# All expert slots gathered ahead of the first expert of a two-block network in fp32 on one NeuronCore

## The reference, cut to what matters

```python
probs = jax.nn.softmax(h @ router_w, axis=-1)            # 16 experts in 4 groups
best_group = jnp.argmax(group_score, axis=-1)            # one group for each token
# two experts of that group, with weights that sum to one -> combine
for e in range(N_EXPERTS):
    he = (jax.nn.silu(h @ w_gate[e]) * (h @ w_up[e])) @ w_down[e]
    out = out + combine[:, e:e + 1] * he
```

## Time and profile before

| | |
|---|---|
| median of 3 runs | 1371.65 us (1367.9 to 1377.59) |
| the profiled execution's own time | 1371.72 us |
| its span | 1370.4 us |
| the small gather | 975.57 to 981.43 us |
| gate sums, slot weights and up sums of the first expert | 981.43 to 1006.57 us |
| the large gather | 1006.57 to 1013.65 us |

### The profile page before, as it was taken

One profiled execution on the slowest core, in us unless ns is written; L12 is line 12 of the kernel. 1 busy time (PEld: TensorE's weight loads), 2 busy tenths in 40 slices (PEclk: granted clock), 3 DMA queues, 4 the chain that ended last, 5 costly groups with the idle time before them and its releaser, 6 DMA issues.

```text
span 1370.4 us, 20186 instructions
## 1 busy us (share of the span) xinstructions
PE 1296.8 (95%) x7932; PEld 1162.0 (85%) x7932; DVE 1021.1 (75%) x1456; ACT 707.8 (52%) x977; POOL 0.4 (0%) x5
## 2 busy tenths in 40 slices
PE   6988999999999999999999899999899999999996
PEld 6877899999888888999998688988788878878775
DVE  5667777777677897878887858775758679688695
ACT  3433444554358873554454544332557567566564
POOL 0000000000000000000000000000000000000000
PEclk9978999999999999999999999999899999999998
DMA  8628788686376766767771732220458869788781
GB/s 339 261 64 325 268 324 304 241 310 238 130 297 256 256 236 253 263 229 255 268 249 52 248 106 77 93 74 1 175 170 314 303 231 341 253 291 298 232 302 67
DMA packets 82688, 308.20 MB, mean 225 GB/s; under 512 B 9313, under 2 KB 9569, under 8 KB 81825
## 3 DMA queue, kind: packets, MB, share of 16 engines
q1 hardware_dynamic: 80352, 292.59, 59.4%
q10 hardware_dynamic: 2240, 14.31, 2.7%
HBM read 305.82 MB, written 1.05 MB: 224 GB/s over the span
## 4 chain that ended last, share of the span: by engine, by line
PE 69%; DVE 18%; DMA 7%; ACT 4%; issue 2%; ACTq 0%; SPq 0%; DVEq 0%
PE ps L468 68%; DMA ring<-stream 5%; DVE w_low L427 4%; DVE junk L427 3%; ACT w_high L427 1%; DMA ring<-moe 1%; DVE ti L427 1%; DVE rs L427 1%; DVE x L427 1%; DVE hsc L427 1%; DVE t_two L427 1%; PE ps L1138 1%; DVE x_low L427 1%; DVE y_experts L427 1%; ACT t_two L427 1%
## 5 line engine op out<-in xcount | busy, mean ns | idle before, releaser
L427 DVE TENSOR_TENSOR w_low<-ring,w_high 128x1024 fp32r<-128x1024 f32 x368 | 442.2, 1222 | 140.1 <-ACT w_high L427 138.3
L427 ACT ACTIVATE w_high<-ring 128x1024 fp32r<-128x1024 f32 x368 | 386.1, 1058 | 300.4 <-PE ps L468 173.9
L468 PE MATMUL ps<-x_high,w_high 128*128 128x256 f32 (+1 forms) x816 | 239.1, 293 | 18.6 <-DVE x_low L427 12.0
L468 PE MATMUL ps<-x_high,w_low 128*128 128x256 f32 (+1 forms) x816 | 235.9, 289 | 0.0
L468 PE MATMUL ps<-x_low,w_high 128*128 128x256 f32 (+1 forms) x816 | 235.5, 289 | 0.0
L427 DVE CUSTOM_DVE_ANT_0 junk<-ring,cond 128x1024 f32<-128x1024 f32 x137 | 167.1, 1223 | 39.6 <-DMA ring<-stream 30.9
L468 PEld LDWEIGHTS ps<-x_high,w_high 128*128 128x128 f32 x816 | 155.8, 191 | 25.9 <-issue 12.0
L468 PEld LDWEIGHTS ps<-x_low,w_high 128*128 128x128 f32 x816 | 155.8, 191 | 1.6
L468 PEld LDWEIGHTS ps<-x_high,w_low 128*128 128x128 f32 x816 | 155.2, 190 | 1.7
L468 PE MATMUL ps<-h_high,w_high 128*128 128x256 f32 x512 | 144.7, 283 | 7.1 <-DVE h_low L427 4.8
L468 PE MATMUL ps<-h_high,w_low 128*128 128x256 f32 x512 | 144.7, 283 | 0.0
(11 more groups left out here) (324 smaller groups left out, 1962.1 us busy)
## 6 DMA issues: line engine op xcount, KB each, us to landing
ring<-stream SPq DMA_DIRECT2D x364, 512.0 KB, 5.3
ring<-moe SPq DMA_DIRECT2D x192, 512.0 KB, 4.8
gw<-gw ACTq DMA_DIRECT2D x1, 3840.0 KB, 16.0
tab_two<-tab ACTq DMA_DIRECT2D x1, 2824.0 KB, 15.4
cond<-cvec ACTq DMA_DIRECT2D x2, 512.0 KB, 5.4
x<-xT ACTq DMA_DIRECT2D x1, 1024.0 KB, 11.7
ctx_first<-ctxT ACTq DMA_DIRECT2D x1, 1024.0 KB, 4.9
ctx<-ctxT ACTq DMA_DIRECT2D x1, 1024.0 KB, 4.9
```

The source lines that it names most:

```text
L427: return op(*a, **k).then_inc(self.sem, by)
L468: return pe.matmul(out, stationary, moving, start=start, stop=stop, skip_group_check=True)
```

## The change

PE does the large gather directly after the small one, and only then the first gate sums, which now wait for all 12 copies of either kind. ScalarE and VectorE take the eight copies of the large gather directly behind the four of the small one, and split the first four weight pieces in between, one after every second copy of the large gather, where before they split one after each copy of the small one. `rows_of_slots` stands behind the second gate piece of the first expert instead of the first. The waits for `scat` and `cw` that stood ahead of the large gather are gone; `products` waits for `cw` in its place. Numbers of instructions are as before on each engine.

```diff
@@ -1073,13 +1073,14 @@
     def rows_of_slots():
 
         pe.wait_ge(s.diag, 2)
-        pe.wait_ge(s.xg_high, 2)
+        pe.wait_ge(s.xg_high, 12)
         for b in range(2):
             ins = mm(PS[:, 5, b * P:(b + 1) * P], m.ONES, m.DIAG[:, b, :], True, True)
         ins.then_inc(s.db_mm, 1)
 
     def weights_of_slots():
         pe.wait_ge(s.comb_w, 1)
+        pe.wait_ge(s.xg_low, 12)
         for i in range(5):
             for b in range(2):
                 ins = mm(PS[:, 7, 4 * i:4 * i + 4], m.ONEHOT[:, b, i * P:(i + 1) * P].bitcast(F32), m.ROUT[:, 848 + 4 * b:852 + 4 * b], b == 0, b == 1)
@@ -1087,8 +1088,6 @@
 
     def other_tokens():
 
-        pe.wait_ge(s.scat, 5)
-        pe.wait_ge(s.cw, 1)
         for k in range(KT):
             pe.wait_ge(s.xg_high, 4 + max(k - 1, 0))
             tokens(PS[:, 4 + k % 2, 0:CAP - 256], 0, k, slice(256, CAP)).then_inc(s.xg_mm, 1)
@@ -1102,12 +1101,9 @@
         pe.wait_ge(s.w_low, split_upto(w + 1))
         for a, tile in enumerate(tiles_of(p)):
             for k in (2 * n, 2 * n + 1):
-                if p == 0 and kind == "g" and a == 0 and k % 2 == 0:
-                    pe.wait_ge(s.xg_high, n + 1)
-                    pe.wait_ge(s.xg_low, n + 1)
-                if p == 1 and kind == "g":
-                    pe.wait_ge(s.xg_high, 4 + k + 1)
-                    pe.wait_ge(s.xg_low, 4 + k + 1)
+                if p == 0 and kind == "g" and (n, a) == (0, 0):
+                    pe.wait_ge(s.xg_high, 12)
+                    pe.wait_ge(s.xg_low, 12)
                 slots = slice(tile * P, (tile + 1) * P)
                 ins = mm3(PS[:, (0 if kind == "g" else 2) + a, :], (m.XGH[:, k, slots], m.XGL[:, k, slots]), weight(w, (k % 2) * 512, 512), k == 0, k == KT - 1)
         ins.then_inc(s.used, 1)
@@ -1122,7 +1118,7 @@
                     pe.wait_ge(s.y_add, Y_SUMS[p - 4])
         for n in range(first, last):
             hidden(p, "g", n)
-            if p == 0 and n == 0:
+            if p == 0 and n == 1:
                 rows_of_slots()
             if p in SCATTERS:
                 scatter(SCATTERS[p], n)
@@ -1173,10 +1169,10 @@
                     ins = mm(out, m.YS[n][:, blk], m.SCAT[:, i + 1, :], n == 0, n == 1)
         ins.then_inc(s.sc_mm, 1)
 
+    other_tokens()
     gate(0, 0, 4)
     weights_of_slots()
     up(0)
-    other_tokens()
     for p in range(NE):
         if p < NE - 1:
             head = 1 if EXPERTS[p + 1][0] == 0 else 2
@@ -1613,7 +1609,11 @@
     for r in range(4):
         act.wait_ge(s.xg_mm, 2 * r + 1)
         A(m.XGH[:, 2 * r:2 * r + 2, 0:256], PS[:, XG_BANKS[r][0], :].rearrange("p (k s) -> p k s", k=2), ACT.Copy, s.xg_high, apart=True)
-        high_upto(W_MOE + r + 1)
+    for k in range(KT):
+        act.wait_ge(s.xg_mm, 8 + 2 * k + 1)
+        A(m.XGH[:, k, 256:CAP], PS[:, 4 + k % 2, 0:CAP - 256], ACT.Copy, s.xg_high, apart=True)
+        if k % 2:
+            high_upto(W_MOE + k // 2 + 1)
 
     def signs(p):
         for a in range(len(tiles_of(p))):
@@ -1652,9 +1652,6 @@
     high_upto(W_MOE + 8)
     signs(0)
     high_upto(W_MOE + 12)
-    for k in range(KT):
-        act.wait_ge(s.xg_mm, 8 + 2 * k + 1)
-        A(m.XGH[:, k, 256:CAP], PS[:, 4 + k % 2, 0:CAP - 256], ACT.Copy, s.xg_high, apart=True)
     for p in range(NE):
         w = MOE_AT[p, "d", 0] - 4
         high_upto(w + 5)
@@ -2362,12 +2359,16 @@
     def first_low(r):
         vv.wait_ge(s.xg_mm, 2 * r + 2)
         op(vv.tensor_copy, m.XGL[:, 2 * r:2 * r + 2, 0:256], PS[:, XG_BANKS[r][1], :].rearrange("p (k s) -> p k s", k=2), inc=s.xg_low, apart=True)
-        low_upto(W_MOE + r + 1)
 
     first_max(ML, NE, EX, st[:, 34:36], TM)
     op(vv.scalar_tensor_tensor, ML, EX, -3e30, ML, ALU.mult, ALU.add)
     for r in range(4):
         first_low(r)
+    for k in range(KT):
+        vv.wait_ge(s.xg_mm, 8 + 2 * k + 2)
+        op(vv.tensor_copy, m.XGL[:, k, 256:CAP], PS[:, 6 + k % 2, 0:CAP - 256], inc=s.xg_low, apart=True)
+        if k % 2:
+            low_upto(W_MOE + k // 2 + 1)
     first_max(ML, NE, E2, st[:, 36:38], TM)
     op(vv.tensor_tensor, EX, EX, E2, ALU.add)
     op(vv.tensor_tensor, EX, EX, PR, ALU.mult)
@@ -2387,6 +2388,8 @@
 
     def products(p):
         vv.wait_ge(s.used, MOE_AT[p, "u", 3] + 1)
+        if p == 0:
+            vv.wait_ge(s.cw, 1)
         for a, tile in enumerate(tiles_of(p)):
             vv.wait_ge(s.silu, tiles_upto(p - 1) + a + 1)
             if p > 0:
@@ -2428,9 +2431,6 @@
             add_branch(d, PS[:, LAST_BANKS[r] if i == 3 else 6 + r % 2, (d % 2) * 256:(d % 2 + 1) * 256], m.MOD[:, 136 + d:137 + d])
 
     low_upto(W_MOE + 12)
-    for k in range(KT):
-        vv.wait_ge(s.xg_mm, 8 + 2 * k + 2)
-        op(vv.tensor_copy, m.XGL[:, k, 256:CAP], PS[:, 6 + k % 2, 0:CAP - 256], inc=s.xg_low, apart=True)
     products(0)
     for p in range(NE):
         w = MOE_AT[p, "d", 0] - 4

```

## The result

The changed kernel takes 1375.66 us (median of 20 runs, 1371.91 to 1381.27), the one before 1370.74 us (20 runs, 1367.5 to 1377.59). The ratio is 1.0036, 95% interval 1.0026 to 1.0046, which is 3.6 to 6.3 us more: a small loss, but clear of the noise. The profiled execution took 1376.15 us, its span is 1374.9 us.

What follows compares the result with a forecast made beforehand. PE was taken to bound the kernel (busy 95% of the span, 69% of the chain that ended last). The terms -7.08 + 10.1 + 0.7 = +3.7 us gave 1375.4 us from 1371.72, with a range of 1370.5 to 1380.5.

Steps and rivals of the forecast that it cites:

- Part A: Large gather leaves its old place between first up sums and second gate, wholly on PE's path: -7.08 us.
- Part B: Large gather ahead of the first gate, which waits until VectorE finishes eight copies and three splits: +10.1 us.
- Part C: Hand-over from first to second expert: without the gather's cover, PE waits for products before the transposes: +0.7 us.
- Parts at nothing: Later `scat` operations, router's small operations, `rows_of_slots`, the `cw` wait and later first four splits: no cost.
- Rival 1: Clock falls in the new gather's pauses and stays low past the gate's start: 1377 to 1379 us; chance 0.27.
- The rule of the Trainium skill: Cycling through PSUM banks with small pauses between matmul groups can swing the clock; first gate sums would start slow.
- Rival 2: VectorE's splits and copies hide under PE, so the large gather runs at PE's pace: 1371.2 to 1371.8; chance 0.09.
- Rival 3: Expert weight stream falls behind in one-tile experts, PE waits a few times: +4 to +6, 1380 us; chance 0.07.
- signs of being wrong: Gate before 989 or after 994, PEclk under 1.00 after 991, or ScalarE's one-tile `ring<-moe` wait much over 1 us.

Runs made afterwards that it cites:

- e6: Kernel before, large gather in its old place, ScalarE and VectorE making the split of the second gate's last piece behind the eight copies; ratio 1.0000.
- e4: Changed kernel, with VectorE doing each of the three low splits between the large gather's copies an extra time into spare memory; ratio 1.0078.
- e2: Changed kernel, with VectorE making all eight copies of the large gather first and the four low splits behind them; ratio 1.0024.
- e3: Changed kernel, with VectorE making the first expert's products ahead of the low split of the second gate's last piece; ratio 1.0032.
- e1: Changed kernel, with the first gate sums waiting for 4 copies of either kind instead of 12; ratio 1.0020.
- e5: Changed kernel with the edits of e1 and e3 together; ratio 1.0029.
- e10: e1 profiled once more, unchanged, to see whether its low clock comes back; one run, 1377.67 us.
- e9: e5 with the 20 slot-weight matmuls made in three portions behind the first gate sums and first two up pieces; ratio 1.0007 (0.9985 to 1.0029).
- e7: Kernel before, with 15 and 16 fill matmuls of 128x128 where PE waits for the router; ratio 0.9993.
- e8: Kernel before with the edits of e6 and e7 together; ratio 0.9981 (0.9966 to 0.9995).

## Why the prediction was right

The forecast was 1375.4 us, +3.7; measured were 1375.66 and +4.9, with +3.6 to +6.3 in the interval. So the forecast difference lies at the low end of the interval. That the time itself fits within 0.3 us is luck: the forecast started from three runs whose median, 1371.65, lay 0.9 above that of the twenty.

- **Part A**, -7.08 us: the gather left, and up sums and second gate join without a gap.
- **Part B**, +10.1 us: measured 16.00 - 5.86 = 10.14. That it fits to 0.04 is partly luck: 0.35 of it is a small gather slowed by the clock (with that of e6 part B is 9.77), and PE waited another 0.21 for ScalarE's `xg_high` ahead of the large gather, which the sum leaves out. The mechanism holds. The first split waited for ScalarE 0.56 us (0.75 forecast), the pauses before low rounds were 0.73 and 0.39 (0.5 to 0.9 forecast, so the second is a little under), and the last wait is VectorE's. That it is VectorE's queue was only argued then; e4 shows it (3.53 us for three operations of 1.14 more), and e2 shows what is next in line.
- **Part C**, +0.7 us: measured 7.25 - 6.48 = 0.77; e3 takes it away.
- **Parts at nothing**: 25.25 against 25.14 us for the first expert's sums. `scat` and the router's small operations cost nothing.
- **Rival 1**, the clock: PEclk is 1.00 from 983.41 to 992.99 us and behind it. The rule of the Trainium skill (TensorE: Matmul & The Clock Gate, section "A second HAM failure mode: psum-queue depth-cycling") was weighed there; with pauses of 0.16 to 1.39 us the trace does not bear it out, and in e4, with pauses of 1.87, 0.27 and 2.43 us, the clock does swing. My 0.27 for it cannot be judged from one outcome. The place was incomplete: in e1, e4, e5 and e10 the clock fell behind the slot weights, where I had put nothing.
- **Rival 2**, splits and copies hidden: e2 and e6 show that it takes moving the splits; in the changed order VectorE has 2.1 us of work for 1.4 us of PE.
- **Rival 3**, the stream: ScalarE waited 1.8 us more for it, PE not at all. ScalarE waiting "for much more than 1 us" was one of my signs of being wrong; 2.8 us is such a wait, and it cost nothing, so the sign was badly chosen. PE waiting for a split would have been the one to look for.

What stays open: the median says 4.9 us with 3.6 as its lower end, and the stretch gives 3.94 from the small gather, 2.93 from the router on, and 3.57 with the clock ahead of the gate alike. In the profile of the kernel before, the clock fell ahead of the router's counts, which took 5.69 us to the small gather, where the changed kernel and e1 to e6 have 4.67 to 4.68. Each kernel has one profile, so whether its other runs had the clock in the same place is not known, and 1 to 2 us of the median's difference are not assigned. The medians of the kernel before vary from 1370.7 to 1371.8 between sets.

## What to carry to other kernels

A block of work that is moved ahead of the sums it was hiding under costs what the slowest queue that serves it takes, not the matmuls: count the copies and splits that VectorE has between its first and its last result, and compare with the gap that goes at the old place. Look also for what stood in the shadow of the moved block; here a split and two products that nobody had waited for came out into the open. Before moving a block, look at what it waits for where it stands; putting one split behind the copies took the pauses out of the old place.

## What the runs showed of the hardware

The clock can fall though the profile shows PE busy all the while. Behind a row of 20 matmuls of 4 columns (2.2 us, PE busy) that followed 11.7 us of full gate sums, it stood at 0.50, the 1.2 GHz level, for about 3 us in e1, e5 and e10, and cost 1.5 us; in e4 it did so too, behind 13.1 us of gate sums. In three portions among wide matmuls (e9, one profile) it did not. In the kernel before, the changed one, e2, e3, e6, e7 and e8 the same row did no harm, so the row alone is not enough, and what else it takes is open. The Trainium skill (TensorE: Matmul & The Clock Gate, section "Why this matters for your kernels") advises against long idle gaps of PE between bursts of matmuls; the rows of e10 show that a stretch with no gap is not enough.
